# Weight panels that arrive in the place of their own remainder

## The chip, the cores and the metric

One core of a Trainium2 chip. The metric is the time of one execution on the device, in microseconds, as the median of several runs.

## What is computed

Two networks of two layers each, one behind the other, over 256 tokens of width 1024, in float32, batch 1. Every weight matrix is read once, from HBM. Cut to what matters:

```
# first network, layer 0            # layer 1
x += s5_mixer(rms_norm(x))          x += attention(rms_norm(x), k, v) @ w_o
x += conv_ffn(rms_norm(x))          x += conv_ffn(rms_norm(x))
kv = rms_norm(x) @ kv_w
# s5_mixer: h @ w_in, a recurrence over time by groups, y = gelu(...),
#           z = y @ w_glu;  z[:, :1024] * sigmoid(z[:, 1024:])
# conv_ffn: g, u = split(h @ w_up)  (2 x 2816);  (silu(conv3(g)) * u) @ w_down

# second network, layers i = 0, 1
x = layernorm(ALPHA * x + 0.5 * swiglu(x))
x = layernorm(ALPHA * x + mixer(x))    # x @ w_in (7696 columns), window attention and
                                       # a gated delta rule, two branches, w_out
x = layernorm(ALPHA * x + 0.5 * swiglu(x))
# swiglu: gate, up = split(x @ w13);  (silu(gate) * up) @ w2
```

## The kernel before

**Panels.** `plan` cuts all weight matrices into panels of 4 k-tiles (512 rows) by 512 columns of float32, 1 MB each, in the order in which they are used; the sixth panel of each column of a down projection has only 2 k-tiles. The gemms in their order are ssm_in (panels 0 to 3), glu (4 to 11), up0, down0 (FFN 0), q, k, v, o, up1 and down1 (FFN 1), then for each layer i of the second network up and down of FFN 2 + 2i, win, brA, brB, wo, and up and down of FFN 3 + 2i. A panel whose 512 columns lie together comes in one transfer ("straight"); where gate and value columns are paired (glu, up of the first network and of each FFN) it comes in two of half the size.

**Splitting.** A matmul takes operands rounded to float32r, so each operand is split into a rounded part and the remainder, and TensorE makes three products: hi by hi, hi by lo and lo by hi (`product`, L2067 to L2069, and L2292 in the up projections). For a weight panel ACT makes w_hi (`split_hi`, L761), DVE makes w_lo = raw - w_hi (`split_lo`, L1282). Only panels 0 to 3 are used as they arrive, in full float32 (L2388); for them POOL counts lo_ready on (L687 to L689).

**Places and waits.** There are RAW = 2 arrival places (`raw`), and SPL = 3 places each for w_hi and w_lo. SP issues the loads in panel order (L646; L648 and L649 for the two halves) and waits before panel p until the remainder of p-2 is made (lo_ready, L639 and L640). `split_hi(p)` waits for the arrival of p and until TensorE has used p-3 (panel_used, L757 to L759), `split_lo(p)` for w_hi of p. TensorE waits for lo_ready and counts panel_used after a panel's last product. In the programs of ACT and DVE, the split of panel p+3 is written just behind the work that belongs to panel p (L770 to L780 and the like), so the order of splits and other work on these engines is fixed by hand.

```
act.wait_ge(raw_loaded[p % RAW], 32 * (p // RAW + 1))
if p >= SPL:
    act.wait_ge(panel_used, p - SPL + 1)
```

**The end of a gemm.** The last two panels of a gemm that is followed by a norm (glu, o, wo, and down) are used by token halves (`by_halves`, L2159 on): all products for the first 128 tokens, then all for the second 128, and panel_used counts only in the second half. So both panels come free close to the end. ACT then has in its program split_hi of the second and third panel of the next gemm (L+2 and L+3, where L is the last panel of the gemm that ends), and behind them `tsplit`, which scales the transposed, normalized tokens into the operands xT of the next gemm (L800, L802; L785 in the variant that copies only). TensorE makes the transposes that tsplit reads (L2216, L2227) and waits for xT before the first products of the next gemm (L2083). After down1, down3 and wo (`hold=True`) the split of L+3 is written between the two halves of tsplit.

**The output of the SSM mixer** comes in four quarters (q = 0 to 3) around the start of the glu gemm. For each, TensorE transposes (L2487) and ACT copies to `Bm` (L987), TensorE multiplies (L2497), ACT applies gelu (L991) and rounds into xT_hi (L998), DVE makes the rest (`output_rest(q)`, L1640), and TensorE multiplies the first column of glu with it (L2509, panels 4 and 5). `split_hi(6)` stands behind quarter 2 (q == 2), ahead of quarter 3's copy; `split_hi(7)` opens the glu gemm on ACT.

## Time and profile before

| what | us |
|---|---|
| median of 3 runs | 2101.35 (2100.43 to 2105.58) |
| the profiled execution | 2100.68 |
| its span | 2098.9 |
| PE busy | 2050.8 (98%) |
| DVE busy | 1425.1 (68%) |
| ACT busy | 1053.1 (50%) |
| POOL busy | 86.7 (4%) |
| panel loads, queue 1 of the DMA engines | 49.2% of 16 engines' span |

The span runs from the first to the last instruction of one execution that the hardware profiler took; its time on the device is 1.8 us longer. An engine's share is of the whole span, and says little of a single stage. Idle time of an engine other than TensorE costs nothing unless TensorE waits behind it. In a timeline row the bracket gives how long the engine was idle before the instruction and what released it.

### The profile page before, as it was taken

To read this page: it belongs to the slowest core of one execution; us is meant where nothing else is said; L and a number is where in the kernel's file an instruction comes from. 1 tells how busy PE (TensorE), PEld (TensorE's weight loads), DVE (VectorE), ACT (ScalarE), POOL (GpSimd) and SP (SyncE) were. 2 spreads that over 40 slices of the span, in tenths; PEclk is the share of its full clock that TensorE was granted. 3 is DMA by queue.
4 is the path that set the end of the run, shared out by engine and by line. 5 is a ranking of instruction groups with operands and counts; after the bars stand their busy time and mean duration, and the time that the engine had idled before them with its cause. 6 is when DMAs were issued, how large, how long until landed. Compare 5 with 4: busy or idle time off the path is not lost.

```text
span 2098.9 us, 33501 instructions
## 1 busy us (share of the span) xinstructions
PE 2050.8 (98%) x14464; PEld 1791.9 (85%) x14464; DVE 1425.1 (68%) x1636; ACT 1053.1 (50%) x1245; POOL 86.7 (4%) x101
## 2 busy tenths in 40 slices
PE   8899999999999999999999999999999999899998
PEld 8878888989888898997778789888889977788887
DVE  8967766567765664876677766476569576677654
ACT  5545654655643553556544455345435564444542
POOL 1000000000000000220000000000003100000000
PEclk9999999999999999999999999999999999999999
DMA  8156555436656655564312565656546543135653
GB/s 194 14 191 191 184 191 171 152 110 188 192 192 191 203 190 189 171 220 129 124 42 95 171 217 183 198 182 200 190 158 209 195 130 103 43 121 183 199 191 130
DMA packets 259699, 342.40 MB, mean 163 GB/s; under 512 B 23373, under 2 KB 169382, under 8 KB 259552
## 3 DMA queue, kind: packets, MB, share of 16 engines
q1 hardware_dynamic: 253984, 328.90, 49.2%
q0 software_dynamic: 2896, 9.15, 1.4%
q10 hardware_dynamic: 2672, 2.22, 0.6%
q8 instruction: 114, 1.87, 0.4%
q14 instruction: 33, 0.27, 0.0%
HBM read 338.14 MB, written 2.10 MB: 162 GB/s over the span
## 4 chain that ended last, share of the span: by engine, by line
PE 89%; DVE 7%; ACT 2%; issue 1%; DMA 1%; POOL 0%; SPq 0%; DVEq 0%; ACTq 0%
PE trp L2292 16%; PE acc L2292 13%; PE acc L2067 12%; PE acc L2069 12%; PE acc L2068 12%; PE trp L2067 3%; PE acc L2083 2%; PE acc L2238 2%; PE trp L2069 2%; PE trp L2068 2%; PE acc L2132 1%; PE acc L2388 1%; PE acc L2766 1%; PE trp L2771 1%; PE acc L2090 1%
## 5 line engine op out<-in xcount | busy, mean ns | idle before, releaser
L1282 DVE TENSOR_TENSOR w_lo<-raw,w_hi 128x2048 fp32r<-128x2048 f32 (+1 forms) x312 | 704.5, 2259 | 381.1 <-ACT w_hi L761 379.6
L761 ACT ACTIVATE w_hi<-raw 128x2048 fp32r<-128x2048 f32 (+1 forms) x312 | 586.1, 1879 | 473.4 <-PE acc L2069 196.3
L2292 PE MATMUL trp<-xT,w_hi 128*128 128x512 f32 x960 | 228.2, 390 | 0.0
L2292 PEld LDWEIGHTS trp<-xT,w_hi 128*128 128x128 f32 x960 | 178.2, 188 | 35.7
L2067 PE MATMUL acc<-w_hi,hT_hi 128*128 128x512 f32 x528 | 205.5, 389 | 0.0
L2068 PE MATMUL acc<-w_lo,hT_hi 128*128 128x512 f32 x528 | 205.5, 389 | 0.0
L2069 PE MATMUL acc<-w_hi,hT_lo 128*128 128x512 f32 x528 | 205.4, 389 | 0.0
L2067 PE MATMUL acc<-xT,w_hi 128*128 128x256 f32 x704 | 199.6, 283 | 0.0
L2068 PE MATMUL acc<-xT,w_hi 128*128 128x256 f32 x704 | 199.2, 283 | 0.0
L2069 PE MATMUL acc<-xT,w_lo 128*128 128x256 f32 x704 | 199.2, 283 | 0.0
L2292 PE MATMUL acc<-xT,w_hi 128*128 128x512 f32 x768 | 182.5, 390 | 0.0
L2292 PEld LDWEIGHTS acc<-xT,w_hi 128*128 128x128 f32 x768 | 142.7, 188 | 28.6
L2068 PEld LDWEIGHTS acc<-xT,w_hi 128*128 128x128 f32 x704 | 135.1, 192 | 0.3
L2067 PEld LDWEIGHTS acc<-xT,w_hi 128*128 128x128 f32 x704 | 135.1, 192 | 0.3
L2069 PEld LDWEIGHTS acc<-xT,w_lo 128*128 128x128 f32 x704 | 135.1, 192 | 0.0
L2292 PEld LDWEIGHTS trp<-xT,w_lo 128*128 128x128 f32 x960 | 119.4, 192 | 2.5 <-DVE w_lo L1282 0.2
L2292 PE MATMUL trp<-xT,w_lo 128*128 128x256 f32 x960 | 120.8, 283 | 0.0
L2069 PEld LDWEIGHTS acc<-w_hi,hT_lo 128*128 128x128 f32 x528 | 99.1, 188 | 20.6
L2067 PEld LDWEIGHTS acc<-w_hi,hT_hi 128*128 128x128 f32 x528 | 99.2, 188 | 20.4
L2068 PEld LDWEIGHTS acc<-w_lo,hT_hi 128*128 128x128 f32 x528 | 99.2, 188 | 20.3
L2067 PE MATMUL trp<-w_hi,xT 128*128 128x512 f32 x256 | 104.7, 409 | 0.8 <-issue 0.8
L2069 PE MATMUL trp<-w_hi,xT 128*128 128x512 f32 x256 | 100.0, 391 | 0.0
(460 smaller groups left out, 3325.7 us busy)
## 6 DMA issues: line engine op xcount, KB each, us to landing
raw<-in_ffn_w SPq DMA_DIRECT2D x184, 512.0 KB
raw<-in_w_in SPq DMA_DIRECT2D x60, 1024.0 KB
raw<-in_ffn_w_up SPq DMA_DIRECT2D x88, 512.0 KB
raw<-in_ffn_w SPq DMA_DIRECT2D x40, 1024.0 KB
raw<-in_ffn_w_down SPq DMA_DIRECT2D x20, 1024.0 KB
raw<-in_ssm_w_glu SPq DMA_DIRECT2D x16, 512.0 KB
raw<-in_kv_w SPq DMA_DIRECT2D x8, 1024.0 KB
raw<-in_w_branch_a SPq DMA_DIRECT2D x8, 1024.0 KB
```

The lines of the kernel that those rows point to most:

```text
L761: A(w_hi[:, p % SPL, 0:kt, :], raw[:, p % RAW, 0:kt, :], ACT.Copy).then_inc(hi_ready, 1)
L1282: V_.tensor_tensor(w_lo[:, p % SPL, 0:kt, :], raw[:, p % RAW, 0:kt, :], w_hi[:, p % SPL, 0:kt, :].bitcast(F32), ALU.subtract).then_inc(lo_ ...
L2067: mm(out, ah, bh, start=first, stop=False, skip_group_check=True)
L2068: mm(out, ah, bl, start=False, stop=False, skip_group_check=True)
L2069: return mm(out, al, bh, start=False, stop=last, skip_group_check=True)
L2083: mm(out[:, n], w[:, p % SPL, k, n * P:n * P + P], src[0][:, k0 + k, :], start=i == k == 0 and w is w_hi and n % 2 == 0, stop=False, skip_ ...
L2090: ins = mm(out[:, n], w_hi[:, p % SPL, kk, n * P:n * P + P], src[1][:, k0 + kk, :], start=False, stop=i == len(gemms[name][j]) - 1 and kk ...
L2132: mm(out[:, t], src[0][:, k0 + k, t * P:t * P + P], w[:, p % SPL, k, :], start=i == k == 0 and w is w_hi, stop=False, skip_group_check=True)
L2238: ins = mm(out[:, t], src[:, 4 * b + k, t * P:t * P + P], w[:, ps[b] % SPL, k, :], start=first and k == 0, stop=last and k == PK - 1, skip ...
L2292: ins = mm(places(out[n // 2][:, n % 2]), weights[:, p % SPL, k, n * P:n * P + P], tokens_of(k0 + k), start=first and k == 0, stop=last an ...
L2388: ins = mm(out[:, n], raw[:, p % RAW, k, n * P:n * P + P], xf[:, k0 + k, :], start=k0 + k == 0 and n % 2 == 0, stop=k0 + k == KT - 1, skip ...
L2766: ins = mm(a[:, h * P:h * P + P], left[:, h, :], right[:, h, :], start=n == 0, stop=n == len(terms) - 1, skip_group_check=True)
```

## The change

There are now four places (SPL = 4) for w_hi and w_lo, and no arrival buffers of their own: `raw` is laid over the memory of `w_lo`, so a panel arrives where its own remainder is later written, and DVE subtracts in place. The memory in SBUF is the same in sum: 2 + 3 + 3 places before, 4 + 4 after. AHEAD = 3 keeps the distance between a panel's use and the split behind it, so the order of the programs stays. The waits change:

- SP loads panel p when TensorE has used p-4 (before: when DVE has made the remainder of p-2). Panels 0 to 3 are loaded without a wait (before: 0 and 1).
- ACT's split_hi waits for the arrival alone, in `arrived(p)` (before: arrival and the use of p-3). DVE's wait is the same.
- There are four arrival semaphores in place of two.

And two splits are moved: split_hi(6) on ACT from behind quarter 2 to behind quarter 3, split_lo(6) on DVE behind output_rest(3).

```diff
-RAW, SPL = 2, 3
+SPL, AHEAD = 4, 3
...
-        raw = sb("raw", [P, RAW, PK, PN])
         w_hi = sb("w_hi", [P, SPL, PK, PN], F32R)
+        arrivals = ExitStack()
+        raw = sb("raw", [P, SPL, PK, PN], F32, arrivals)
+        arrivals.close()
         w_lo = sb("w_lo", [P, SPL, PK, PN], F32R)
...
+        def arrived(p):
+
+            return raw_loaded[p % SPL], 32 * (p // SPL + 1)
...
-                if p >= RAW:
-                    sp.wait_ge(lo_ready, p - RAW + 1)
+                if p >= SPL:
+                    sp.wait_ge(panel_used, p - SPL + 1)
...
-                act.wait_ge(raw_loaded[p % RAW], 32 * (p // RAW + 1))
-                if p >= SPL:
-                    act.wait_ge(panel_used, p - SPL + 1)
+                act.wait_ge(*arrived(p))
                 kt = panels[p][3]
-                A(w_hi[:, p % SPL, 0:kt, :], raw[:, p % RAW, 0:kt, :], ACT.Copy).then_inc(hi_ready, 1)
+                A(w_hi[:, p % SPL, 0:kt, :], raw[:, p % SPL, 0:kt, :], ACT.Copy).then_inc(hi_ready, 1)
...
                     for p in ps[:-1]:
-                        split_hi(p + SPL)
+                        split_hi(p + AHEAD)
...
                 A(xT_hi[:, 2 * q:2 * q + 2, :], y_gelu[q % 2], ACT.Copy).then_inc(sem("yhi_ready"), 1)
-                if q == 2:
-                    split_hi(6)
+            split_hi(6)
...
             output_rest(2)
+            output_rest(3)
             split_lo(6)
-            output_rest(3)
```

Everywhere else SPL becomes AHEAD in the distance of a split, and raw's index becomes p % SPL.

The first place is ACT around output quarter 3 and the start of glu. Before:

```order
L987 ACTIVATE Bm<-trp0 128x2x16x16 [waits chunks_filled]
L991 ACTIVATE tb<-acc0 128x512 [waits across_done,ylo_ready]
L998 ACTIVATE xT<-tb 128x2x256 [waits act_steps]
L761 ACTIVATE w_hi<-raw 128x2048 [waits panel_used,raw_loaded0]
L987 ACTIVATE Bm<-trp1 128x2x16x16 [waits chunks_filled]
L991 ACTIVATE Kbd<-acc0 128x512 [waits across_done,ylo_ready]
L998 ACTIVATE xT<-Kbd 128x2x256 [waits acc_freed0]
L761 ACTIVATE w_hi<-raw 128x2048 [waits panel_used,raw_loaded1]
```

The same place of ACT in the changed kernel:

```order
L991 ACTIVATE Bm<-trp0 128x2x16x16 [waits chunks_filled]
L995 ACTIVATE tb<-acc0 128x512 [waits across_done,ylo_ready]
L1002 ACTIVATE xT<-tb 128x2x256 [waits act_steps]
L991 ACTIVATE Bm<-trp1 128x2x16x16 [waits chunks_filled]
L995 ACTIVATE Kbd<-acc0 128x512 [waits across_done,ylo_ready]
L1002 ACTIVATE xT<-Kbd 128x2x256 [waits acc_freed0]
L765 ACTIVATE w_hi<-raw 128x2048 [waits raw_loaded2]
L765 ACTIVATE w_hi<-raw 128x2048 [waits raw_loaded3]
```

The rounding of panel 6 (the first L761 before) has moved behind the whole of quarter 3, next to that of panel 7, and neither waits for panel_used.

The second place is ACT at the end of down2, where the mixer of the second network begins; the last two w_hi rows are the panels L+2 and L+3. Before:

```order
L761 ACTIVATE w_hi<-raw 128x1024 [waits panel_used,raw_loaded1]
L761 ACTIVATE w_hi<-raw 128x2048 [waits panel_used,raw_loaded0]
L761 ACTIVATE w_hi<-raw 128x2048 [waits panel_used,raw_loaded1]
L761 ACTIVATE w_hi<-raw 128x2048 [waits panel_used,raw_loaded0]
L802 ACTIVATE xT<-trp0,cols 128x256 [waits turned]
```

In the changed kernel:

```order
L765 ACTIVATE w_hi<-raw 128x1024 [waits raw_loaded1]
L765 ACTIVATE w_hi<-raw 128x2048 [waits raw_loaded2]
L765 ACTIVATE w_hi<-raw 128x2048 [waits raw_loaded3]
L765 ACTIVATE w_hi<-raw 128x2048 [waits raw_loaded0]
L806 ACTIVATE xT<-trp0,cols 128x256 [waits turned]
```

Nothing has moved here; the roundings wait for the arrival alone, and tsplit (L802, now L806) still stands behind both.

The third place is SP's queue at the first panels of glu. Before:

```order
L624 DMA dng<-in_dn_norm_g 128x256
L648 DMA raw<-in_ssm_w_glu 128x4x256 [waits lo_ready]
L649 DMA raw<-in_ssm_w_glu 128x4x256
L648 DMA raw<-in_ssm_w_glu 128x4x256 [waits lo_ready]
L649 DMA raw<-in_ssm_w_glu 128x4x256
```

In the changed kernel:

```order
L630 DMA dng<-in_dn_norm_g 128x256
L654 DMA raw<-in_ssm_w_glu 128x4x256 [waits panel_used]
L655 DMA raw<-in_ssm_w_glu 128x4x256
L654 DMA raw<-in_ssm_w_glu 128x4x256 [waits panel_used]
L655 DMA raw<-in_ssm_w_glu 128x4x256
```

The order of the loads is the same; what releases each of them is now TensorE, not DVE.

## Rows read from the trace of the kernel before

**Rows 1.** The page: busy time by engine, and the group of split_lo.

```profile
PE 2050.8 (98%) x14464; PEld 1791.9 (85%) x14464; DVE 1425.1 (68%) x1636; ACT 1053.1 (50%) x1245; POOL 86.7 (4%) x101
...
L1282 DVE TENSOR_TENSOR w_lo<-raw,w_hi 128x2048 fp32r<-128x2048 f32 (+1 forms) x312 | 704.5, 2259 | 381.1 <-ACT w_hi L761 379.6
```

**Rows 2.** The waits of TensorE: microseconds in total, times, the longest.

```profile
PE acc L2497 <- ACT Bm L987: 3.4, 3, 3.0
```

**Rows 3.** The chain of waits, 160 to 240: start, microseconds, what.

```profile
182.30 11.11 PE acc L2292 x64
```

**Rows 4.** Timeline: start, duration, engine, line, operation, [idle before <-releaser]. SP's queue, 105.

```profile
105.30 0.37 SPq L648 DMA_DIRECT2D raw<-in_ssm_w_glu  x1
```

**Rows 5.** The timeline of ACT, 109 to 118.

```profile
112.71 1.91 ACT L761 ACTIVATE w_hi<-raw 128x2048 fp32r<-128x2048 f32 x1 [3.67 <-DMA raw<-in_ssm_w_glu]
114.53 0.58 ACT L987 ACTIVATE Bm<-trp 128x512 f32<-128x512 f32 x1
...
117.05 0.63 ACT L998 ACTIVATE xT<-Kbd 128x512 fp32r<-128x512 f32 x1
```

**Rows 6.** The timeline of PE, 109 to 122.

```profile
111.09 1.07 PE L2509 MATMUL acc<-w_lo,xT 128*128 128x512 f32 x4
115.16 1.16 PE L2497 MATMUL acc<-cst,Bm 128*128 128x128 f32 x8 [3.00 <-ACT Bm L987]
...
121.62 0.39 PE L2067 MATMUL acc<-w_hi,xT 128*128 128x512 f32 x1
```

**Rows 7.** Loads of two panels and their roundings: SP's queue, then ACT, 1140 to 1151.

```profile
1141.61 0.39 SPq L646 DMA_DIRECT2D raw<-in_w_branch_b  x1
1143.82 0.39 SPq L646 DMA_DIRECT2D raw<-in_w_out  x1
...
1146.63 1.92 ACT L761 ACTIVATE w_hi<-raw 128x2048 fp32r<-128x2048 f32 x1 [6.36 <-DMA raw<-in_w_branch_b]
1149.32 1.92 ACT L761 ACTIVATE w_hi<-raw 128x2048 fp32r<-128x2048 f32 x1 [0.78 <-DMA raw<-in_w_out]
```

**Rows 8.** A panel in two transfers: SP's queue at 163, ACT at 168.

```profile
163.56 0.37 SPq L648 DMA_DIRECT2D raw<-in_ffn_w_up  x1
...
168.84 1.92 ACT L761 ACTIVATE w_hi<-raw 128x2048 fp32r<-128x2048 f32 x1 [7.01 <-DMA raw<-in_ffn_w_up]
```

**Rows 9.** The end of down2: ACT and PE, 836 to 844.

```profile
837.38 1.92 ACT L761 ACTIVATE w_hi<-raw 128x2048 fp32r<-128x2048 f32 x1 [4.88 <-PE acc L2069]
...
842.27 1.93 ACT L802 ACTIVATE xT<-trp,cols 128x256 fp32r<-128x256 f32 x4 [0.51 <-PE trp L2216]
...
842.98 0.71 PE L2083 MATMUL acc<-xT,w_hi 128*128 128x256 f32 x4
```

**Rows 10.** The end of down0: ACT, 341 to 347.

```profile
341.32 1.92 ACT L761 ACTIVATE w_hi<-raw 128x2048 fp32r<-128x2048 f32 x1 [4.88 <-PE acc L2069]
...
346.35 0.84 ACT L800 ACTIVATE qx<-trp,cols 128x256 fp32r<-128x256 f32 x2 [0.52 <-PE trp L2216]
```

**Rows 11.** The end of down4: ACT, 1555 to 1561.

```profile
1555.74 1.92 ACT L761 ACTIVATE w_hi<-raw 128x2048 fp32r<-128x2048 f32 x1 [4.88 <-PE acc L2069]
...
1560.63 0.56 ACT L802 ACTIVATE xT<-trp,cols 128x256 fp32r<-128x256 f32 x1 [0.29 <-PE trp L2216]
```

**Rows 12.** The end of the attention output: ACT, 462 to 470.

```profile
462.71 1.92 ACT L761 ACTIVATE w_hi<-raw 128x2048 fp32r<-128x2048 f32 x1 [6.24 <-PE acc L2069]
...
469.10 1.21 ACT L800 ACTIVATE xT<-trp,cols 128x256 fp32r<-128x256 f32 x3 [1.76 <-PE trp L2216]
```

**Rows 13.** The end of the GLU: ACT, 151 to 160.

```profile
151.80 1.92 ACT L761 ACTIVATE w_hi<-raw 128x2048 fp32r<-128x2048 f32 x1 [2.33 <-PE acc L2069]
...
158.80 1.57 ACT L800 ACTIVATE xT<-trp,cols 128x256 fp32r<-128x256 f32 x4 [2.15 <-PE trp L2216]
```

**Rows 14.** The end of down1: ACT, 651 to 660.

```profile
651.62 1.92 ACT L761 ACTIVATE w_hi<-raw 128x2048 fp32r<-128x2048 f32 x1 [4.88 <-PE acc L2069]
...
658.61 1.09 ACT L785 ACTIVATE xT<-trp 128x512 fp32r<-128x512 f32 x2 [2.23 <-PE trp L2227]
```

More of the change, by code:

```diff
@@ L352, in build @@
         ftab_d = nc.dram_tensor("ftab_d", (HEADS, P, P), F32, kind="Internal").ap()
-        raw_loaded = [sem(f"raw_loaded{i}") for i in range(RAW)]
+        raw_loaded = [sem(f"raw_loaded{i}") for i in range(SPL)]
         hi_ready, lo_ready, panel_used = sem("hi_ready"), sem("lo_ready"), sem("panel_used")
@@ L771, in gemm @@
                     for p in ps[:-1]:
-                        split_hi(p + SPL)
+                        split_hi(p + AHEAD)
                     evacuate(j, place(name, j))
@@ L776, in gemm @@
                     elif not hold or j < len(gemms[name]) - 1:
-                        split_hi(ps[-1] + SPL)
+                        split_hi(ps[-1] + AHEAD)
                     if after:
@@ L827, in gate @@
                             ins.then_inc(sem("tap_ready"), 1)
-                        split_hi(gemms[f"up{f}"][j][-1] + SPL)
+                        split_hi(gemms[f"up{f}"][j][-1] + AHEAD)
                         act.wait_ge(sem("conv_ready"), 2 * hn + 2)
@@ L1013, in _ @@
                 if t:
-                    split_hi(gemms["glu"][3][0] + SPL)
+                    split_hi(gemms["glu"][3][0] + AHEAD)
                     wait_filled(act, u)
                 A(hbuf[:, 1, t], A2(u)[:, t, PN // 2:PN], ACT.Sigmoid).then_inc(sem("glu_gate"), 1)
-            split_hi(gemms["glu"][3][1] + SPL)
+            split_hi(gemms["glu"][3][1] + AHEAD)
             tsplit("ffn0", *gain_of("ffn0"))
@@ L1059, in _ @@
             softplus(0)
-            split_hi(gemms["v0"][0][0] + SPL)
+            split_hi(gemms["v0"][0][0] + AHEAD)
             values_out(0)
-            split_hi(gemms["v0"][0][1] + SPL)
+            split_hi(gemms["v0"][0][1] + AHEAD)
             softplus(1)
-            split_hi(gemms["v1"][0][0] + SPL)
+            split_hi(gemms["v1"][0][0] + AHEAD)
             values_out(1)
-            split_hi(gemms["v1"][0][1] + SPL)
+            split_hi(gemms["v1"][0][1] + AHEAD)
             for i in range(8):
@@ L1170, in beside @@
                         gate_columns(j)
-                    split_hi(p + SPL)
+                    split_hi(p + AHEAD)
                 def decay_exp(q):
@@ L1217, in _ @@
                         A(Lc[side(b), t], L[side(b), t, :, side(b)], ACT.Copy).then_inc(sem(f"L_blocks{t}"), 1)
-                split_hi(p + SPL)
+                split_hi(p + AHEAD)
                 A(gates[:, :, 0, :], gates[:, :, 0, :], ACT.Sigmoid).then_inc(sem("gate_a_ready"), 1)
@@ L1226, in _ @@
                     if lv == 1:
-                        split_hi(gemms[f"brA{i}_0"][0][0] + SPL)
+                        split_hi(gemms[f"brA{i}_0"][0][0] + AHEAD)
                 for t in range(TT):
@@ L1233, in _ @@
                     A(Ys[side(1), t], small_bank(trp[t])[side(1)], ACT.Copy).then_inc(sem(f"Y_copied{t}"), 1)
-                split_hi(gemms[f"brA{i}_0"][0][1] + SPL)
+                split_hi(gemms[f"brA{i}_0"][0][1] + AHEAD)
                 def copied(d, to):
@@ L1281, in split_lo @@
                 kt = panels[p][3]
-                V_.tensor_tensor(w_lo[:, p % SPL, 0:kt, :], raw[:, p % RAW, 0:kt, :], w_hi[:, p % SPL, 0:kt, :].bitcast(F32),
+                V_.tensor_tensor(w_lo[:, p % SPL, 0:kt, :], raw[:, p % SPL, 0:kt, :], w_hi[:, p % SPL, 0:kt, :].bitcast(F32),
                                  ALU.subtract).then_inc(lo_ready, 1)
@@ L1294, in gemm @@
                         if p <= last - hold:
-                            split_lo(p + SPL)
+                            split_lo(p + AHEAD)
                     if not first or j:
@@ L1298, in gemm @@
                     if not inside and ps[-1] <= last - hold:
-                        split_lo(ps[-1] + SPL)
+                        split_lo(ps[-1] + AHEAD)
                     if after:
                         after(j, place(name, j))
-                late.extend(range(last - hold + 1 + SPL, last + 1 + SPL))
+                late.extend(range(last - hold + 1 + AHEAD, last + 1 + AHEAD))
             def late_splits():
@@ L1479, in gate @@
                                 .then_inc(sem("conv_ready"), 1)
-                        split_lo(gemms[f"up{f}"][j][-1] + SPL)
+                        split_lo(gemms[f"up{f}"][j][-1] + AHEAD)
                     dve.wait_ge(sem("gate_ready"), hn + 1)
@@ L1868, in _ @@
                         scores(n)
-                    split_lo(side_panel(i, n)[2] + SPL)
+                    split_lo(side_panel(i, n)[2] + AHEAD)
                     if n < 8:
@@ L1880, in _ @@
                 decay(2)
-                split_lo(side_panel(i, 10)[2] + SPL)
+                split_lo(side_panel(i, 10)[2] + AHEAD)
                 decay(3)
@@ L1967, in _ @@
                         scaled_keys(lv - 3)
-                        split_lo((side_panel(i, 11)[2], gemms[f"brA{i}_0"][0][0])[lv - 3] + SPL)
+                        split_lo((side_panel(i, 11)[2], gemms[f"brA{i}_0"][0][0])[lv - 3] + AHEAD)
                 for t in range(TT):
@@ L1975, in _ @@
                     dve.sem_inc(*freed(u))
-                split_lo(gemms[f"brA{i}_0"][0][1] + SPL)
+                split_lo(gemms[f"brA{i}_0"][0][1] + AHEAD)
                 u = use[f"dl{i}"] + 1
@@ L2024, in _ @@
                     V_.tensor_tensor(g, g, trp[2 + t][:, :], ALU.mult).then_inc(sem("a1_gated"), 1)
-                late.extend(p + SPL for p in gemms[f"brA{i}_1"][0])
+                late.extend(p + AHEAD for p in gemms[f"brA{i}_1"][0])
                 tsplit(f"delta_{i}")
@@ L2387, in inputs @@
                         for n in range(4):
-                            ins = mm(out[:, n], raw[:, p % RAW, k, n * P:n * P + P], xf[:, k0 + k, :], start=k0 + k == 0 and n % 2 == 0,
+                            ins = mm(out[:, n], raw[:, p % SPL, k, n * P:n * P + P], xf[:, k0 + k, :], start=k0 + k == 0 and n % 2 == 0,
                                      stop=k0 + k == KT - 1, skip_group_check=True)
```

26 lines of the change are left out of this document (13 added, 13 removed).

## The prediction, made before the changed kernel ran

> **What bounds the kernel now.** The page comes first: the reader is to see that TensorE is busy for 2050.8 of 2098.9 us, and that DVE and ACT, which split the weight panels, are far from full [rows 1]. So a change of buffers can give back only what TensorE waits, and can cost whatever new wait it puts on TensorE's path. The second view is the list of what TensorE waits for. It names no panel load and, in the stream, no w_hi or w_lo. One entry bears on the change: 3.4 us in three waits for ACT's copy Bm at L987, of which one alone is 3.0 us [rows 2]. One entry of the list is longer, a single wait for the first small load of the kernel, which SP issues ahead of every panel. The chain of waits shows the steady stream: 64 matmuls in 11.11 us for the two panels of a column, 5.56 us per panel, back to back [rows 3].
>
> The timeline shows what made the 3.0 us wait. SP issues the load of panel 6 only at 105.30, when DVE is done with the remainder of panel 4 [rows 4]. ACT has split_hi(6) in its program ahead of the copy for output quarter 3, idles 3.67 us for that load, rounds from 112.71, and only then, at 114.53, makes the copy [rows 5]. TensorE stops after 111.09 + 1.07 and starts again at 115.16 [rows 6].
>
> **The sum: the gain.** After the change split_hi(6) stands behind the output loop. The copy at L987 no longer follows it; TensorE goes on at 115.16 - 3.00 = 112.16. Each later instruction of the quarter moves up by 3.00: ACT's last operation of the loop (L998) starts at 114.05 in place of 117.05 and ends at 114.7. What is late next is panel 6 itself, which the second GLU column needs at 121.62 - 3.00 = 118.62 [rows 6]. Its load is no issue now: its place was panel 2's, used long before. split_hi(6) takes 1.9 (to 116.5) and DVE's split_lo(6) takes 2.26 by its mean [rows 1], to 118.8. That is 0.2 after 118.62. DVE does output_rest(3) before, but that ends while ACT still rounds. **Gain 3.0 - 0.2 = 2.8 us.** Bounds: nothing, if something else holds that copy, and 3.0.
>
> **The sum: the loss.** The arrival place of panel p is now the place of w_lo(p-4), so its load waits until TensorE has used panel p-4, and ACT's wait for panel_used becomes a wait for the arrival, which comes a whole load later. In the stream this is covered: SP issues at the use of p-4, TensorE needs p three panels later, 3 x 5.56 = 16.7 us, and load, rounding and remainder take 5.0 + 1.9 + 2.3 = 9.2. Where a gemm ends it is not. Its last two panels are used by token halves, so the use of the last but one (call it L-1) comes one token half of the last panel before the end: 5.56 / 2 = 2.8 us, or 1.4 after down, whose last panel has two k-tiles in place of four. And ACT's program has split_hi(L+2), split_hi(L+3) and then the operations that feed the next gemm (L800, L802). Before, both panels had arrived, or nearly. Now the load of L+3 is only issued at that use.
>
> The price of a load: issued 1141.61, ACT starts on it at 1146.63, so 5.02; the next, issued 2.2 us behind it, 1143.82 to 1149.32, 5.50 [rows 7]. A panel that comes in two transfers, issued 163.56, 168.84: 5.28 [rows 8]. I take 5.02 for straight panels and 5.28 for paired ones, since L+3 is the first of the two and rows 7 show the first undisturbed. Behind the load, ACT's next operation begins 1.82 after split_hi's start (112.71 to 114.53 in rows 5).
>
> - down2 to the second mixer: the use of L-1 is at 837.38 (where ACT was released before), so 837.38 + 5.02 + 1.82 = 844.22 for L802, against 842.27; TensorE starts 0.71 behind it, at 842.98, with nothing between [rows 9]: +1.95.
> - down0 to the query gemm: 341.32 + 6.84 = 348.16 against 346.35 [rows 10]: +1.8.
> - down4 to the last mixer: 1555.74 + 6.84 = 1562.58 against 1560.63 [rows 11]: +1.95.
> - attention output to ffn1, a paired panel: 462.71 + 7.10 = 469.81 against 469.10 [rows 12]: +0.7.
> - GLU to ffn0: 151.80 + 7.10 = 158.90 against 158.80 [rows 13]: +0.1.
> - down1, and two more like it (down3, wo0), hold one split back between the halves of the transposes. Use at 651.62, plus 5.02 and 1.9 is 658.5; L785 starts at 658.61 anyway [rows 14]: 0, at most 0.2 each.
>
> **Loss 6.5 us.** By the rows 3.7 remain: 2100.68 (the profiled execution) + 6.5 - 2.8 = **2104.4**. The median shown is 2101.35, 0.7 above that execution, so against it this is +3.0, or 0.15%.
>
> One rule speaks on the price of the load. The row has 5.02 us for a panel of 1 MB. The Trainium skill (SBUF — State Buffer, section on the DMA setup-cost knee) gives about 2 us fixed plus the bytes at 436 GB/s, which is an estimate of 4.4 us by that page. With it each of the boundaries would be 0.6 shorter, the loss about 4.0, the net +1.2 and the time 2101.9. The rows of this kernel decide.
>
> Costed at nothing: the first loads. Panels 2 and 3 are now issued without a wait and TensorE waits for no panel there; they could push one of the small loads of the start back by up to half a load, 2.5 us, or bring nothing. DVE writes w_lo over its own input; L1282's mean of 2.26 would have to grow by some 7 us to come out of the 16.7 - 9.2 of slack. Behind SP's new wait stand only the next panels and one load of masks that the attention part uses much later; POOL's waits name the same panels as before (AHEAD is 3, as SPL was).
>
> **Rivals.**
> A, forecast, chance 0.62: gain 2.8, loss 6.5, own range 2102 to 2107.5 (loads 5.0 to 5.5 at four boundaries, 0.2 at each of three more, gain 2.8 to 3.0).
>
> B, the boundaries cost next to nothing, chance 0.13: ACT's rounding of L+3 would have to be hidden, because the load is quicker or the use of L-1 is counted earlier than ACT's row shows. Then only the gain is left, 2100.7 - 2.8 = 2097.9. For it speaks only that the margins are within 2 us; against it that ACT was released in rows 9 to 11 exactly by TensorE's last product, after 4.88 us of idleness.
>
> C, slower side, chance 0.17: **two loads share the engines**. At each boundary the load of L+4 is now issued 1.4 or 2.8 us behind that of L+3, where before the loads stood apart. If L+3 takes 7.4 us, as the load of panel 6 did (105.30 to 112.71, rows 4 and 5), the five plain boundaries cost 2.4, 2.4, 2.4, 2.1 and 2.1 more, and two of those with a held split, 651.62 + 7.4 + 1.9 = 660.9 against 658.61, 2.3 each (counted for two of the three): 16.0 us more, 2120.4. From 0.5 us more on each of these seven loads, 5.5 in place of 5.02, the whole is slower by over 0.3%. Against it: rows 7, where the first of two loads 2.2 us apart was not slowed. For it: there the second did take half a microsecond more, and 1.4 is closer than 2.2.
>
> D, the stream itself, chance 0.04: before, two arrivals waited beside three split panels, five ahead; now four in all. If a load is caught by the small gain and bias loads, 9.2 could grow past 16.7 only with a load of over 12 us; none of that length stands in the trace. It would give some 10 us more, 2114.
>
> E, the early load of panel 6 is not what matters, chance 0.04: if the copy Bm at L987 is held by something else that ends at the same time, the gain falls away and the loss stays, 2107.2. Against it: in rows 5 the copy starts as soon as the rounding lets ACT go, with no wait noted.
>
> **How the numbers follow.** The likeliest time is A's, 2104. The range takes in B below and most of what lies between A and C: 2097 to 2112; C's full price and D are left out. This kernel can be told from no change by about 0.3%, 6.3 us, so from 2095.0 down or 2107.7 up. Faster: only B with a gain I have not seen, 0.05. Slower: C, D and A's upper end with E, 0.20. The same: 0.75.
>
> **What would show it.** In the profile after: the wait of 3.0 us at L2497 gone from TensorE's list; ACT waiting for a DMA of in_w_in and in_attn_w_q at the end of down0, down2 and down4, with split_hi at 5.0 us behind the use and L802 some 1.8 to 2 us later than before against the last product of down; panel loads after a boundary between 5.0 and 5.5 us. Wrong would be: those loads at 6 or more (C), L802 at its old distance (B), waits for w_lo inside the stream (D), or a second GLU column that waits over 0.5 us for w_lo(6).

## The result, and the profile after

The changed kernel takes 2109.96 us (median of 5 runs, 2107.44 to 2113.15), the kernel before beside it 2101.35. The ratio is 1.0041, with a 95% interval of 1.0023 to 1.0060: slower, by more than the forecast's 0.15%, and with a wider spread. The profiled execution took 2107.44 us, 6.8 more than that of before, and it is the shortest of the five; the mean granted clock was 0.997 in it and 0.994 to 0.996 in the others, which took 1.6 to 5.7 us longer.

TensorE's busy time on the page of the changed kernel answers to rows 1. It has not grown, so the sum of what was lost is waiting. (The sum hides that each trace has two short stretches at the lower clock in TensorE's work: before from 75.7 and from 1813.1, after from 845.7 and from 1569.3. More on them below.)

```profile
PE 2050.0 (97%) x14464; PEld 1791.8 (85%) x14464; DVE 1424.2 (68%) x1636; ACT 1049.5 (50%) x1245; POOL 80.2 (4%) x101
```

In the list of what TensorE waits for (microseconds in total, times, the longest), the 3.4 us of rows 2 have shrunk to the last line here, and the lines above it are new or have grown; before, no wait for ACT's tsplit (L806, L804) was in the list, and the first line stood at 2.8:

```profile
PE acc L2774 <- issue: 4.9, 3, 2.6
PE acc L2086 <- ACT xT L806: 4.3, 2, 2.2
...
PE acc L2086 <- ACT qx L804: 1.9, 1, 1.9
...
PE acc L2086 <- ACT xT L804: 0.9, 2, 0.7
...
PE acc L2500 <- ACT Bm L991: 0.4, 2, 0.2
```

Instruction by instruction, the two traces have the same order on TensorE, so the start of each in one can be subtracted from that in the other. Where that difference steps, time was lost or won. Within a few microseconds of each place (times of before):

| place in the trace of before | step, us | what |
|---|---|---|
| 110 | -3.1 | the wait for Bm, gone |
| 120 | +0.3 | second GLU column, w_lo(6) |
| 346, end of down0 | +1.9 | wait for qx |
| 469, end of attention output | +0.7 | wait for xT |
| 658, end of down1 | +0.2 | first products of up2 |
| 842, end of down2 | +2.0 | wait for xT |
| 844 to 849 | +1.5 | the products behind that wait, slow |
| 1068 to 1101, delta rule | +2.1 | "issue" wait in the small products |
| 1560, end of down4 | +2.1 | wait for xT |
| 1562 to 1567 | +1.5 | again slow products |
| all other places together | -2.5 | among them -1.9 at 71 to 79 and -1.5 at 1800 to 1830, where the clock was low in the trace of before and not in this one, +1.6 at 96 (a wait for DVE, 3.00 in place of 1.37), and +0.2 at the end of the GLU |

The last row is what is left to make the 6.7 us between the two spans; it also has -0.55 in the first 12 us and small steps near 1190 and 1204. So between these two executions the lower clock nearly cancels: 3.0 us behind the two ends, and some 3 us at 75 to 79 and 1813 to 1817 that only the trace of before has.

**The gain**, as it looks after (ACT, then TensorE; answers to rows 5 and 6):

```profile
107.88 0.63 ACT L1002 ACTIVATE xT<-tb 128x512 fp32r<-128x512 f32 x1
108.77 0.60 ACT L991 ACTIVATE Bm<-trp 128x512 f32<-128x512 f32 x1 [0.26 <-PE trp L2490]
...
113.23 0.63 ACT L1002 ACTIVATE xT<-Kbd 128x512 fp32r<-128x512 f32 x1
113.77 3.70 ACT L765 ACTIVATE w_hi<-raw 128x2048 fp32r<-128x2048 f32 x2
...
111.46 1.05 PE L2500 MATMUL acc<-cst,Bm 128*128 128x128 f32 x8
...
118.14 0.47 PE L2070 MATMUL acc<-w_hi,xT 128*128 128x512 f32 x1 [0.17 <-DVE w_lo L1285]
```

The copy Bm (L991) starts at 108.77 with 0.26 of idle time, and TensorE's L2500 follows the product before it at 111.46 with no wait. Both splits stand behind the loop, at 113.77. The second GLU column waits 0.17 for w_lo(6).

**The loss**, at the end of down2 (SP's queue, ACT, TensorE; answers to rows 9):

```profile
837.01 1.75 SPq L652 DMA_DIRECT2D raw<-in_w_in  x2
...
842.14 1.91 ACT L765 ACTIVATE w_hi<-raw 128x2048 fp32r<-128x2048 f32 x1 [4.74 <-DMA raw<-in_w_in]
843.96 3.73 ACT L806 ACTIVATE xT<-trp,cols 128x256 fp32r<-128x256 f32 x8
...
844.65 0.71 PE L2086 MATMUL acc<-xT,w_hi 128*128 128x256 f32 x4 [2.05 <-ACT xT L806]
845.20 0.65 PE L2086 MATMUL acc<-xT,w_lo 128*128 128x256 f32 x4
845.68 1.03 PE L2086 MATMUL acc<-xT,w_hi 128*128 128x256 f32 x4
846.50 1.05 PE L2086 MATMUL acc<-xT,w_lo 128*128 128x256 f32 x4
847.36 1.90 PE L2093 MATMUL acc<-xT,w_hi 128*128 128x256 f32 x8
849.07 0.66 PE L2086 MATMUL acc<-xT,w_hi 128*128 128x256 f32 x4
```

The load of L+3 is issued at 837.01, ACT starts on it 5.13 later, at 842.14, and the first operation of tsplit begins 1.82 behind that, at 843.96. TensorE waits 2.05. But look at the lines behind the wait: four 256-column products take 0.71 and 0.65 us, then 1.03 and 1.05 where they take 0.64 again at 849. The stretches of the same trace (length, busy time of PE, PEld, DVE, ACT and POOL with their counts, then the granted clock, the share of the DMA engines and GB/s) say what that is:

```profile
844.00:845.60 1.60, 0.95 (x8) 0.98 (x9) 0.60 (x3) 1.60 (x5) 0.00 (x0) 1.00 0.17 64
845.60:849.00 3.40, 3.40 (x19) 3.40 (x18) 3.40 (x8) 3.40 (x6) 0.00 (x0) 0.51 0.00 0
849.00:852.00 3.00, 3.00 (x27) 3.00 (x26) 3.00 (x8) 0.49 (x1) 0.00 (x0) 0.98 0.00 0
```

The granted clock was 0.51 from 845.6 to 849, the lower of the two levels, 1.2 GHz in place of 2.4, right behind the stretch in which TensorE stood. At the end of down4 the same happens behind 2.21 us of waiting:

```profile
1570.00:1574.00 4.00, 4.00 (x26) 4.00 (x25) 4.00 (x8) 3.20 (x5) 0.00 (x0) 0.66 0.00 0
```

**The issue wait**, in the delta rule of the first layer (SP's queue, then TensorE):

```profile
1088.23 0.39 SPq L652 DMA_DIRECT2D raw<-in_w_branch_b  x1
...
1095.94 0.21 PE L2774 MATMUL acc<-Ti,qkT 64*64 64x64 f32 x1 [2.59 <-issue]
```

TensorE stands for 2.59 us and no engine releases it. The load of panel 165 started at 1088.23; before, that load started only at 1103. The queue that the page calls q8, kind "instruction", moves 114 packets of 16 KB in the whole execution, one for some 250 of TensorE's instructions (14464 matmuls and as many weight loads). In this part of the trace of before they come 3.8 to 4.7 us apart (1078 to 1108). Here one came at 1085.86, none while the load ran, and the next at 1093.61, when its last bytes moved; TensorE went on at 1095.94. Queues with packets in 1087 to 1093.5, then in 1093.5 to 1094 (packets, MB, share of the engines):

```profile
q1 hardware_dynamic: 522, 1.04, 57.2%
...
q8 instruction: 1, 0.02, 12.1%
```

### The profile page after: what moved, and what is told of

Same layout as the page of the kernel before. It is cut to its first block, busy times and chain, and to the rows that moved or that the text cites. A ratio compares the mean times of both kernels' runs of the same rounds, so it can differ in the third digit from the quotient of the medians.

```text
span 2105.6 us, 33201 instructions
## 1 busy us (share of the span) xinstructions
PE 2050.0 (97%) x14464; PEld 1791.8 (85%) x14464; DVE 1424.2 (68%) x1636; ACT 1049.5 (50%) x1245; POOL 80.2 (4%) x101
## 4 chain that ended last, share of the span: by engine, by line
PE 89%; DVE 6%; ACT 2%; DMA 2%; issue 1%; SPq 0%; DVEq 0%; ACTq 0%
PE trp L2295 16%; PE acc L2295 13%; PE acc L2070 12%; PE acc L2071 12%; PE acc L2072 12%; PE trp L2070 2%; PE acc L2086 2%; PE trp L2071 2%; PE trp L2072 2%; PE acc L2241 2%; PE acc L2135 1%; PE acc L2391 1%; PE trp L2774 1%; PE acc L2769 1%; PE acc L2093 1%
## 5 line engine op out<-in xcount | busy, mean ns | idle before, releaser
L2070 PE MATMUL trp<-w_hi,xT 128*128 128x512 f32 x256 | 104.7, 409 | 0.0
L2071 PE MATMUL trp<-w_lo,xT 128*128 128x512 f32 x256 | 100.0, 391 | 0.0
```

The source lines that it names most:

```text
L2070: mm(out, ah, bh, start=first, stop=False, skip_group_check=True)
L2071: mm(out, ah, bl, start=False, stop=False, skip_group_check=True)
```

## The experiments

Before's own median moved between the three sets of runs (2098.35, 2100.08, 2100.29), so kernels are compared by their ratio to the kernel before on the same chip. It is the one on record, and differs from the ratio of the two medians by up to 0.0007 (e4). 1.0041 stands for the changed kernel throughout.

| kernel | median us | ratio to before | 95% interval | mean granted clock |
|---|---|---|---|---|
| e1_round_behind | 2097.15 | 0.9992 | 0.9983 to 1.0001 | 0.9977 |
| e2_before_move | 2098.84 | 1.0005 | 0.9996 to 1.0014 | 0.9975 |
| e3_after_warm | 2109.14 | 1.0050 | 1.0036 to 1.0063 | 0.9966 |
| e4_before_pad | 2110.34 | 1.0050 | 1.0037 to 1.0063 | 0.9950 |
| e5_after_warm_two | 2107.36 | 1.0029 | 1.0018 to 1.0040 | 0.9973 |
| e6_before_both_moves | 2097.91 | 0.9993 | 0.9984 to 1.0001 | 0.9977 |
| e7_behind_unmoved | 2096.93 | 0.9983 | 0.9974 to 0.9992 | 0.9975 |
| e8_behind_keep_warm | 2097.88 | 0.9988 | 0.9979 to 0.9997 | 0.9980 |
| e9_delta_loads_late | 2094.82 | 0.9975 | 0.9966 to 0.9984 | 0.9976 |
| e10_behind_two_ends | 2100.75 | 1.0005 | 0.9996 to 1.0014 | 0.9969 |

The mean granted clock of the changed kernel is 0.9954 over its five runs.

### e1: the rounding of L+3 behind tsplit

```diff
-            split_hi(gemms["glu"][3][1] + AHEAD)
             tsplit("ffn0", *gain_of("ffn0"))
+            split_hi(gemms["glu"][3][1] + AHEAD)
             ffn(0)
             tsplit("mix1", *gain_of("mix1"), to=qx)
+            split_hi(gemms["down0"][-1][-1] + AHEAD)
...
-            gemm("o", lambda j, u: None)
+            gemm("o", lambda j, u: None, hold=True)
             tsplit("ffn1", *gain_of("ffn1"))
+            split_hi(gemms["o"][-1][-1] + AHEAD)
...
-                gemm(f"down{f}", lambda j, u: None, hold=f >= 1 and f % 2 == 1 and f < 5)
+                gemm(f"down{f}", lambda j, u: None, hold=f < 5)
...
                 tsplit(f"ln0_{i}", *gain_of(f"ln0_{i}"))
+                split_hi(gemms[f"down{2 + 2 * i}"][-1][-1] + AHEAD)
```

> The changed kernel, but at the five plain ends of a gemm (GLU, down0, attention output, down2, down4) the rounding of the fourth panel ahead (L+3) stands behind tsplit on ACT instead of ahead of it. Theory A (the loss is ACT waiting there for a load, and TensorE waiting for ACT, with a lower granted clock behind the two longest waits): the waits of 1.9, 2.05 and 2.2 us at L2086 go, and with them the slow products behind the last two (about 1.5 us each); against the changed kernel 2.1 + 0.7 + 3.5 + 3.9 = about 10 us less, so about 2098 to 2100, 2 to 3 us under the kernel before. Rival (the shorter look-ahead and the new times of the loads cost in the stream and elsewhere, the ends being only where it shows): a part of these waits comes back later, and the time stays above 2104.

Measured 2097.15, ratio 0.9992. Against 1.0041 that is 0.49% or 10.3 us, give or take some 4 us by the two intervals, as Theory A had it; the runs lie within 3.2 us of each other, against 5.7 for the changed kernel. At the end of down2 (ACT, then TensorE):

```profile
840.43 3.75 ACT L806 ACTIVATE xT<-trp,cols 128x256 fp32r<-128x256 f32 x8 [4.51 <-PE trp L2222]
844.03 3.76 ACT L765 ACTIVATE w_hi<-raw 128x2048 fp32r<-128x2048 f32 x2
...
841.14 0.71 PE L2089 MATMUL acc<-xT,w_hi 128*128 128x256 f32 x4
```

tsplit starts with TensorE's transposes, the rounding of L+3 and L+4 comes behind it, and nothing of it returns later: the difference to the trace of before does not step by 0.25 us between 121 and 1089 except by 0.3 at down1. **With the loads starting this late, the order of two operations on ACT was the loss**, not the shorter look-ahead in the stream.

### e2: before, with the move of panel 6 alone

```diff
                 A(xT_hi[:, 2 * q:2 * q + 2, :], y_gelu[q % 2], ACT.Copy).then_inc(sem("yhi_ready"), 1)
-                if q == 2:
-                    split_hi(6)
+            split_hi(6)
...
-            split_lo(6)
             output_rest(3)
+            split_lo(6)
```

> The kernel before (two arrival places, three for the parts), with only the rounding of panel 6 and its remainder moved behind the last output quarter. Theory A (the 3.0 us wait for the copy Bm was ACT standing at the load of panel 6 by program order): the wait goes, panel 6 still arrives at about 112.7, w_hi(6) is ready at 116.5 and w_lo(6) at 118.8, so 2.8 us less than before: 2098.5. Rival (the four places are needed for it, as the panel comes too late for the second GLU column): the wait moves to w_lo(6), and the time is that of the kernel before, 2101.

Measured 2098.84, ratio 1.0005: no gain that could be measured. In its trace the step of -3.1 at 110 is there, and the wait for Bm is off the list. But with two arrival places every later load of the GLU waits for the remainder of the panel two ahead, which is now made later, and the last column waits for w_lo (TensorE):

```profile
143.75 0.47 PE L2066 MATMUL acc<-w_hi,xT 128*128 128x512 f32 x1 [1.09 <-DVE w_lo L1281]
```

So 0.3 and 1.35 of the 3.1 are given back by 142. In this execution TensorE also waited 3.51 us for DVE at 96, which has nothing to do with the move, and behind it the granted clock was 0.50 over 98 to 101; that cost 4.2 us against the trace of before, which had lost 1.9 at 71 to 79 where this one did not. The 1.5 us of the move that should be left are not in the median; the interval reaches from 0.8 under to 2.9 us over the kernel before. Neither theory as put is confirmed: the wait moved, but by half, and what is left is within the noise.

### e3: products without use in the waits

```diff
                     if arriving and j == 0:
+                        if i == 0 and name in ("win0", "win1"):
+                            stay_warm(acc[u % 2], 4)
                         for k in range(kt):
```

> The changed kernel, with four 128x512 products without use (as its stay_warm has them, 0.45 us each) on TensorE between the transposes and the first products of the two mixers' w_in, where it waits 2.05 and 2.21 us. They write the accumulator that the first product overwrites. Theory A (the 1.5 and 1.7 us behind these waits are the granted clock, which fell because TensorE stood still): the granted clock stays at 1.0 there, and the time is 3 us under the changed kernel, 2107 or so, the waits for ACT being as long as before. Rival (the slow products come from something else at that place, such as the weight loads or the memory being read by ACT and DVE at once): no change, 2110, products still at about 0.21 us in place of 0.12.

Measured 2109.14, ratio 1.0050, no better than the changed kernel. I had mis-sized the filler: the four products took 3.60 us, 0.9 each and not 0.45, and the first real product came 0.8 us late at both places. The trace still answers the question (TensorE, then the stretch with its clock):

```profile
842.08 3.60 PE L2196 MATMUL acc<-cst 128*128 128x512 f32 x8
845.12 1.04 PE L2088 MATMUL acc<-xT,w_hi 128*128 128x256 f32 x4
845.99 0.64 PE L2088 MATMUL acc<-xT,w_lo 128*128 128x256 f32 x4
...
845.00:847.00 2.00, 2.00 (x15) 1.67 (x14) 2.00 (x7) 2.00 (x6) 0.00 (x0) 1.00 0.00 1
```

The granted clock is 1.00 behind both waits and the products take 0.64, where the changed kernel had 1.05. What the clock gave, the too long filler took in part: the steps at the two ends are 3.1 and 3.1 us, where the changed kernel had 3.5 and 3.6. As a time, this run settles nothing.

### e4: before, with a delay and no load

```diff
+                if p in (gemms["down2"][-1][-1] + SPL, gemms["down4"][-1][-1] + SPL):
+                    for n in (PK, 1):
+                        step(A(w_hi[:, p % SPL, 0:n, :], raw[:, p % RAW, 0:n, :], ACT.Copy))
+                        step.settle()
                 A(w_hi[:, p % SPL, 0:kt, :], raw[:, p % RAW, 0:kt, :], ACT.Copy).then_inc(hi_ready, 1)
```

> The kernel before, with the rounding of the fourth panel ahead of the ends of down2 and down4 done once in full and once in a quarter more than needed (same data, same place), so that tsplit of the two mixers starts about 2.2 us later with no load under way. Theory A (an idle TensorE of about 2 us there is enough for the lower clock): 2 x 2.2 for the waits and 2 x 1.6 for the clock, about 7.5 us over the kernel before, 2109. Rival (the slow products need the load that runs at the same time, as in the changed kernel): only 2 x 2.2, 2105.7, at a granted clock of 1.0 behind the waits.

Measured 2110.34, ratio 1.0050: 10.5 us over the kernel before by the ratio, 12.0 by the medians, for two waits of 2.44 and 2.24 us that were not there before. Its mean granted clock is 0.9950, that of the kernel before is 0.997 to 0.998. In the profiled execution, the second shortest of its five, the clock fell behind the first of the two waits only (TensorE at both places, then the stretches in and behind each wait):

```profile
846.13 1.19 PE L2087 MATMUL acc<-xT,w_hi 128*128 128x256 f32 x4 [2.44 <-ACT xT L806]
847.12 1.05 PE L2087 MATMUL acc<-xT,w_lo 128*128 128x256 f32 x4
...
1567.88 0.71 PE L2087 MATMUL acc<-xT,w_hi 128*128 128x256 f32 x4 [2.24 <-ACT xT L806]
1568.42 0.64 PE L2087 MATMUL acc<-xT,w_lo 128*128 128x256 f32 x4
...
843.50:846.10 2.60, 0.19 (x2) 0.00 (x1) 0.00 (x0) 2.57 (x4) 0.00 (x0) 0.98 0.00 0
847.00:850.00 3.00, 3.00 (x18) 3.00 (x18) 3.00 (x8) 2.17 (x5) 0.00 (x0) 0.60 0.00 0
1565.50:1567.80 2.30, 0.14 (x2) 0.00 (x0) 0.00 (x0) 2.30 (x3) 0.00 (x0) 1.00 0.00 0
1569.00:1571.00 2.00, 2.00 (x19) 2.00 (x18) 2.00 (x7) 1.92 (x5) 0.00 (x0) 1.00 0.00 0
```

No load ran at either place (a DMA share of 0.00, in the waits and behind them). **The lower clock behind a wait needs no load, and not every such wait gets it**: 2.44 did, 2.24 did not, with the same code around. In the same execution it also fell from 115.5 on, behind the wait of 2.48 us for Bm; the 3.00 of the same wait in the trace of before had no such fall. An estimate from the clocks: the mean clock of the kernel before on this chip is 0.9977, so 0.0027 of 2100 us, 5.7 us, is lost by the clock, and with 4.7 for the waits that is 10.4, near the 10.5 by the ratio. Theory A's 7.5 took two falls in each execution for the whole; by this estimate there are more.

### e5: a filler of the right size

As e3, with `stay_warm(acc[u % 2], 2)`, and for `q` too.

> The changed kernel, now with two products without use, not four (the four took 3.6 us together, longer than the wait), ahead of the first products of q and of both w_in: 1.8 us, inside the waits of 1.9, 2.05 and 2.2 us. Theory A (TensorE standing still lets its clock fall, in some executions at more than one of these places, which is what spreads the changed kernel's runs from 2107 to 2113): granted clock 1.0 behind all three, the runs closer together and at a mean clock of 0.997 to 0.998, the waits for ACT still there; 2104 to 2106. Rival (what spreads the runs lies elsewhere): a median of 2109 and a spread of 6 us as before.

Measured 2107.36, ratio 1.0029, mean clock 0.9973: the clock of the kernel before is nearly back (0.9954 to 0.9973), and 1.2 per mille of time (2.5 us), though the intervals of 1.0029 and 1.0041 overlap. By the ratio it lies 6 us over the kernel before, between Theory A's 2104 to 2106 and the rival's 2109: neither is confirmed. The clock did not fall behind the three waits with a filler; it fell once elsewhere, behind the end of the GLU (0.50 over 157.7 to 161). The spread is 5 us still. Part of it is in this profiled execution, one of the longer ones: the load of L+3 at the end of the attention output (SP, ACT; and the filler at down2):

```profile
463.86 0.37 SPq L654 DMA_DIRECT2D raw<-in_ffn_w_up  x1
...
470.81 1.91 ACT L765 ACTIVATE w_hi<-raw 128x2048 fp32r<-128x2048 f32 x1 [8.17 <-DMA raw<-in_ffn_w_up]
...
846.52 1.88 PE L2196 MATMUL acc<-cst 128*128 128x512 f32 x4
```

463.86 to 470.81 is 6.95 us, where the same load took 5.38 in the profile of the changed kernel, and TensorE waited 2.3 in place of 0.7 there; at the end of the GLU it was 5.8. Whatever a load takes longer now lands on TensorE at these ends. Of 15 such loads at the five ends in three traces, 14 took between 5.04 and 5.82.

### e6: before, with both orders changed

e2 with the rounding of L+3 behind tsplit as in e1 (with SPL for AHEAD).

> The kernel before with its two arrival and three part places, with both moves of program order: the rounding of panel 6 behind the last quarter, and the rounding of L+3 behind tsplit at the five ends. Theory A (before, L+3 had arrived in time, so the second move brings nothing here; the first brings 3.0, of which the GLU gives back 1.4 by a wait for w_lo): as e2_before_move, 2098 to 2099, and 1 to 2 us over e1_round_behind, which is what four places are worth. Rival (the places are worth nothing once the order is right): the same time as e1_round_behind, 2097.

Measured 2097.91, ratio 0.9993. In the trace the wait for w_lo in the GLU is there (0.99, and TensorE 1.3 later behind it), and nothing at the ends. Against e7 on the same chip it is 1.0 us more by the medians and 2.1 by the ratios; the intervals overlap, so once the order is right, what four places are worth is 1 or 2 us and not told apart from nothing.

### e7: panel 6 back where it was

e1, with split_hi(6) and split_lo(6) where the kernel before has them.

> e1_round_behind with split_hi(6) and split_lo(6) where the kernel before has them (behind and ahead of the last quarter's start). Theory A (the 3.0 us came from ACT standing 3.67 us at the load; with four places panel 6 arrives long before): ACT rounds at once, 1.9 us, the copy Bm starts at about 111 in place of 109.2, before TensorE is through with its products at 112; the same time as e1_round_behind within 0.5 us, 2097. Rival (the place in the program is what counts): 1.5 to 3 us over e1_round_behind.

Measured 2096.93, ratio 0.9983, against 0.9992 of e1: at least as good. ACT, then TensorE:

```profile
108.89 1.91 ACT L765 ACTIVATE w_hi<-raw 128x2048 fp32r<-128x2048 f32 x1
110.70 0.57 ACT L991 ACTIVATE Bm<-trp 128x512 f32<-128x512 f32 x1
...
111.94 1.05 PE L2504 MATMUL acc<-cst,Bm 128*128 128x128 f32 x8
```

ACT rounds panel 6 at once at 108.89, the copy Bm follows at 110.70, and TensorE starts L2504 at 111.94 without a wait. **With four places the panel is there early, and the move is not needed.** With three (e2) the move alone also took away the wait for Bm, and the late panel gave half of it back.

### e8: more products ahead of the SSM outputs

```diff
-            keep_warm(30)
+            keep_warm(45)
```

> e1_round_behind with keep_warm(45) in place of keep_warm(30) ahead of the SSM outputs, 15 small products of 0.115 us more, 1.7 us of the 3.4 us that TensorE waits there for DVE. Theory A (the wait of 3.4 us lets the clock fall: products of 0.018 us each ran at 0.031 behind it in two traces): the wait shrinks to 1.7 us, the granted clock stays at 1.0, 1.5 to 2 us less in the executions where it fell, so a median of 2096. Rival (the stage ends with DVE's chain anyway, so the slow products cost nothing): the same median, 2097.

Measured 2097.88, ratio 0.9988 against 0.9992 of e1: not told apart; its runs lie within 3.0 us. This filler was mis-sized too: 45 products took 10.27 us where 30 take 6.92, 3.4 us more and not 1.7. In the profiled execution DVE's result was ready at 97.13 and TensorE, still in the filler, started on it at 100.08, 3 us late; the clock stayed at 1.00 over 97 to 101, where e1 has 0.65, but it had been low earlier (from 73.7). So the run does not decide between the theory and the rival, whose reason (DVE's chain ends the stage) the trace does not show.

### e9: the loads of the delta rule as late as before

e7, with:

```diff
                     sp.wait_ge(panel_used, p - SPL + 1)
+                if any(p in gemms[f"brB{i}"][0] for i in range(DEPTH)):
+                    sp.wait_ge(lo_ready, p - 1)
```

> e7_behind_unmoved, in which SP also waits, before the first two panels of brB (164, 165 and 274, 275), for the remainder of the panel two ahead, as it did in the kernel before: these loads start at about 1097 and 1103 in place of 1069 and 1081, and the same in the second layer. In the traces of all kernels with four places TensorE stands 1.0 to 2.6 us with no engine to wait for ('issue') some 7 us behind the load of 165, in the middle of the delta rule's many small products, and once more in the second layer; those with three places do not have that wait. Theory I (the load takes the DMA engines while TensorE's instructions are to be fetched): that wait goes, 1.3 to 1.8 us less in each layer, 2094 where e7 gave 2096.9, ratio to the kernel before 0.997. Rival (the waits come from the size and place of the program's instructions in memory, not from the loads): they stay, 2097, ratio 0.998.

Measured 2094.82, ratio 0.9975; by the ratios 1.7 us under e7, with overlapping intervals (e7 ends at 0.9974 below, e9 at 0.9984 above), and half way between Theory I's 0.997 and the rival's 0.998. The time alone decides nothing; the trace does. The list of issue waits in that stretch of TensorE is now that of before, the first of them:

```profile
1095.74 0.27 PE L2780 MATMUL acc<-qkT,Ti 64*64 64x64 f32 x1 [1.06 <-issue]
```

The wait that stood at 1088 (1.76 us in e7) and the one at 1806 (2.24) are gone; in the first layer it was 1.75, 1.84 and 1.98 in the traces of e1, e3 and e5. The rival had them stay. The difference to the trace of before steps by +1.0 (1080 to 1110) and +2.2 (1800 to 1810) in e7, and by nothing and -0.3 in e9; e9's execution had come to the delta rule some 1 us later than e7's, by a wait of 3.46 us for DVE at 96 and the clock behind it. In seven traces with four places and early loads, a packet of queue q8 at the load of 165 came 6.6 to 7.8 us after the one ahead of it, in six of them as that load ended (in e8 in its middle); in e9 and those with three places no gap between 1078 and 1108 is over 5.1. Queues with packets in 1080.2 to 1085.7, e7 and then e9:

```profile
q1 hardware_dynamic: 520, 1.04, 56.3%
...
q8 instruction: 2, 0.03, 2.4%
```

An issue wait is not always a load's: the trace of before has one of 1.83 at 1811.51, ahead of any load there, and e9 one of 1.56 at 1808.93. And a part of its price is the clock, which fell behind that wait in e1 (0.50 over 1090 to 1093) and in e3 (0.50 over 1095 to 1098). This is the fastest kernel of the study by its median.

### e10: the order changed at two of the five ends

e1's edit at the ends of down2 and down4 only.

> The changed kernel with the rounding of L+3 behind tsplit only at the ends of down2 and down4, not at those of the GLU, down0 and the attention output. Theory A (each end costs its own wait and what the clock gives back for it): 3.5 + 3.9 us less than the changed kernel in the profiled execution, about 2103, ratio to the kernel before 1.0005 to 1.001, with 2.1 + 0.7 us of waits left. Rival (only the sum of all idle time counts, or the ends of the first network carry as much in the executions that are not profiled): over 2105, ratio 1.0025 or more.

Measured 2100.75, ratio 1.0005, Theory A's number; 0.36% or 7.6 us under the changed kernel, for 7.4 predicted, nearer than the two intervals (some 4 us) can show. In its profile the clock fell at the end of down0, where it had not in that of the changed kernel, behind a wait of the same length (1.86 against 1.88). TensorE:

```profile
347.17 1.20 PE L2087 MATMUL acc<-qx,w_hi 128*128 128x256 f32 x4 [1.86 <-ACT qx L804]
348.16 1.05 PE L2087 MATMUL acc<-qx,w_lo 128*128 128x256 f32 x4
```

## Why the prediction was right in its parts and low in its sum

**Right, by size.** The bound (TensorE's waits) and the place of the gain: 2.8 forecast, 3.1 - 0.3 = 2.8 in the trace. Its reason was half of the matter: the forecast put it down to the move of the rounding, and e7 has it without the move. The ends, in the order of the forecast (down2, down0, down4, attention output, GLU, down1): 1.95, 1.8, 1.95, 0.7, 0.1 and 0 forecast; 2.0, 1.9, 2.1, 0.7, 0.2 and 0.2 measured. The loads of L+3 took 5.13 to 5.49 at the plain ends, for 5.02 and 5.28, which is the small excess. The time lay in the range, though outside that of rival A (2102 to 2107.5), whose mechanism it was; the sign of the sum was right, and e1 and e10 came out at the price of the ends within their intervals once the clock was in it.

**Rule and row.** The load had 5.02 us by the row and an estimate of 4.4 by the Trainium skill (SBUF — State Buffer, section on the DMA setup-cost knee). Measured at the ends were 5.04 and more in every case, so the trace does not agree with the 4.4, and the row was the better price.

**The step that failed** is the one that priced a wait of TensorE at its own length ("down2 to the second mixer: ... +1.95", and the two like it). Behind two such waits the granted clock was 0.51 and 0.66 (means of the stretches above) and the products cost 1.5 us more each. The profiled execution took 2107.44, 3.0 over the 2104.4 of the sum. That this is just the 3.0 of the two falls is chance: there were also +2.1 in the delta rule and 0.6 more at the ends, and -2.7 at the other places. In the executions that were not profiled the clock was lower, and with its mean from 0.997 down to 0.994 the time goes up by 5.7 us. Of the 8.6 us between the medians the clock takes 2.5 by what e5 gave back, with overlapping intervals, and 4.8 by an estimate from the mean clocks (0.9954 against 0.9977 of the kernel before beside e1, of 2100 us). The trace of before could have said so. TensorE, and the stretch behind it:

```profile
74.83 2.79 PE L2348 MATMUL trp<-cst 128*128 128x128 f32 x15 [1.83 <-issue]
...
75.00:80.00 5.00, 5.00 (x26) 4.77 (x27) 4.87 (x6) 3.30 (x12) 0.00 (x0) 0.66 0.01 3
```

A wait of 1.83 us (and one of 1.82 at 71.28), and then a granted clock of 0.66. The same stands behind the 1.83 at 1811.51, with 0.50 over 1813.2 to 1816.4, and not behind the 3.00 at 115.16. I had read the granted clock as a mean (0.998) and not by stretch.

**A second one that was costed at nothing**: the new times of loads away from the ends. I had looked for loads that come too late; these came too early, in the middle of the small products of the delta rule, and TensorE stood up to 2.59 us with nothing to wait for but its own issue; 2.1 us in sum in the first layer. e9 shows that the time of the loads is the cause. The traces also point to the way: the next packet of the instruction queue came only as the load ended, and TensorE went on 2.3 to 2.4 us behind its start (1093.61 to 1095.94 after, 1085.81 to 1088.22 in e7, 1804.55 to 1806.84 in its second layer). That the load holds the packet up is read from these times, and no run tests it by itself. Why the packet does not wait in e9 (load 1096.69 to 1101.37, a packet at 1098.18) stays open.

**Of the rivals**, B (the ends cost nothing) and D (waits in the stream) did not come about. C (two loads share the engines, 7.4 us) did not either as a rule: with the next load issued 1.36 or 2.72 us behind, 14 of 15 were under 5.9; but one of them took 6.95, and such a load now counts. E (the gain falls away, as something else holds the copy Bm) did not come about: the wait of 3.00 is gone after. But its first words, that the early load is not what matters, are turned round by e7: with the panel loaded early the move is not needed.

**The verdict** "the same within 0.3%" had 0.75 and was the wrong one: 0.41%, with an interval that begins at 0.23%. The case that came true was A plus two prices that I had not given it.

**What stays open.** How much of the spread of the changed kernel is the clock and how much late loads: both were seen in profiled executions, and the others can't be looked into. What decides whether the clock falls behind a given wait: 1.86 did and 1.88 did not, and a wait of 3.0 for DVE before 95.95 left it at 1.00 in the changed kernel, while behind 3.44 at the same place in e1 it fell (0.65 over 97 to 101). And why e2's median shows nothing of the 1.5 us that its trace keeps, while e6's does (0.9993).

## What to carry to other kernels

A buffer that is freed by the consumer in place of the splitter moves each load later or earlier; look at both: what now waits behind it in program order at the ends of a stage, and what it newly runs beside. Before buying buffers, see whether the operation that the critical engine waits for stands behind one that nobody needs yet; with the new buffers in place, swapping two lines on ACT was worth 10 us here. That took back a loss that the buffers had brought. The kernel before with the same orders (e6) came to 0.9993, not told apart from no change; with four places 0.9983 (e7), and with the loads of the delta rule held back as well 0.9975 (e9), both clear of no change and not of each other. And count a new wait of TensorE of two microseconds at up to 1.7 times its length (2.05 and 1.5 us behind it), because of the clock; some such waits get no lower clock at all.

## What the runs showed of the hardware that was not expected

- The granted clock can fall to 0.5 behind a wait of TensorE of 1.86 to 2.44 us (0.51 over 845.6 to 849), and behind another of the same length not (1.88, 2.24). With 1.8 us of products without use in the wait it stayed at 1.00 (e5, all three places).
- A product of 128 by 512 in plain float32 takes 0.9 us (3.60 for the four of e3) and stands in the trace as two matmuls; I had read the x4 in the row of stay_warm as four products.
- TensorE's issue can stall for 1.0 to 2.6 us just after a 1 MB load that ran beside a stretch of many small products: packets of the instruction queue that came 4 us apart were 7.75 apart around the load (1085.86 to 1093.61). Stalls of up to 1.83 us also stand in the trace of before with no load beside them (1811.51).
